# A hybrid decoder step on one core: key/value projection and compressed pages as three products of rounded parts

## The reference

```python
def key_side(h):
    kv = (rms_norm(h, kv_norm) @ w_kv).reshape(B, T, 3, 2, N_KV, HEAD_DIM)
    return kv[:, :, 0], kv[:, :, 1], kv[:, :, 2]        # raw rows, stored as outputs too

def seg_proj(seg):                                       # segments of 16 cached rows
    first = jnp.einsum('bsjcgd,cjde->bscge', seg, cmp_w[:, :CMP_STRIDE])
    second = jnp.einsum('bsjcgd,cjde->bscge', seg, cmp_w[:, CMP_STRIDE:])
    return first, second

def compress_blocks(first, second, L):                   # blocks of 32 rows, 16 apart
    blk = first[:, :nc] + second[:, 1:nc + 1] + cbias[:, None, :]
    kc = rms_norm(blk[:, :, 0], k_norm[0])
    return kc, blk[:, :, 1], e_pos
```

## Time and profile before

| | us |
|---|---|
| median of 3 runs | 2643.77 |
| range of the runs | 2643.24 to 2648.64 |
| profiled execution, its own time | 2653.37 |
| its span, first to last instruction | 2651.6 |
| TensorE busy | 2437.2 (92%) |
| VectorE busy | 1385.0 (52%) |
| ScalarE busy | 904.4 (34%) |
| mean granted TensorE clock | 0.948 |

### The profile page before, as it was taken

The page is one execution under the profiler, slowest core; times in us unless marked ns, Lnnn a source line. Parts: engine busy times, 40 slices in busy tenths (PEclk is TensorE's granted clock), DMA queues, the critical chain, the costliest instruction groups (busy, mean ns, idle before and its releaser), DMA issues. The chain is left out here.

```text
span 2651.6 us, 62243 instructions
## 1 busy us (share of the span) xinstructions
PE 2437.2 (92%) x25616; PEld 1985.1 (75%) x25616; DVE 1385.0 (52%) x2833; ACT 904.4 (34%) x2023; POOL 774.1 (29%) x460
## 2 busy tenths in 40 slices
PE   5999799986899999989999898997999978999998
PEld 3777699965799999944544385565766677999998
DVE  7216665536577773022233435774777746777600
ACT  2205344315222121110101145765888822222210
POOL 0001000110267665200000023772222204677641
PEclk8999899967899999999999987997999988999999
DMA  2121000012122223151898310005777612222231
GB/s 106 55 64 57 8 4 12 28 39 90 59 72 79 87 74 119 49 221 47 323 326 280 118 58 1 2 1 185 253 251 251 224 64 67 79 87 79 94 99 61
DMA packets 109448, 276.58 MB, mean 104 GB/s; under 512 B 13657, under 2 KB 14554, under 8 KB 107290
## 3 DMA queue, kind: packets, MB, share of 16 engines
q1 hardware_dynamic: 109210, 273.19, 30.5%
HBM read 264.42 MB, written 16.97 MB: 106 GB/s over the span
## 5 line engine op out<-in xcount | busy, mean ns | idle before, releaser
L319 PE MATMUL ps<-parts 128*128 128x288 f32 x6144 | 815.1, 295 | 7.4 <-POOL parts L288 7.4
L319 PEld LDWEIGHTS ps<-parts 128*128 128x128 f32 x6144 | 814.2, 188 | 8.1 <-POOL parts L288 8.1
L288 POOL TENSOR_TENSOR parts<-kept,parts 128x1024 fp32r<-128x1024 f32 (+1 forms) x120 | 320.7, 2673 | 119.5 <-ACT parts L283 112.3
L293 POOL TENSOR_TENSOR parts<-kept 128x1024 fp32r<-128x1024 f32 (+1 forms) x92 | 191.5, 2081 | 378.2 <-DMA kept<-in_wall 188.6
L1660 PE MATMUL ps<-mix,kept 128*128 128x512 f32 (+1 forms) x544 | 228.4, 579 | 0.3 <-DMA mix<-in_cmp_pool 0.3
L1660 PEld LDWEIGHTS ps<-mix,kept 128*128 128x128 f32 x544 | 101.4, 194 | 120.8 <-issue 119.7
L2292 POOL TENSOR_SCALAR mix<-mix 128x128 f32<-128x128 f32 (+3 forms) x128 | 136.7, 1087 | 71.9 <-DVE mix L2266 71.8
L288 POOL TENSOR_TENSOR query_rounded<-mix,query_rounded 128x1024 fp32r<-128x1024 f32 x8 | 16.0, 2000 | 466.8 <-ACT query_rounded L283 466.8
L2769 POOL TENSOR_TENSOR mix<-mix 128x512 f32<-128x512 f32 x64 | 67.0, 1047 | 252.7 <-ACT mix L2793 197.9
L1599 DVE TENSOR_TENSOR kept<-kept,ps 128x576 f32<-128x576 f32 x16 | 12.1, 756 | 245.9 <-PE ps L319 245.9
L702 PE MATMUL ps<-mix 128*128 128x288 f32 x512 | 126.4, 410 | 2.7 <-DVE mix L507 2.4
(11 more groups left out here) (470 smaller groups left out, 4870.0 us busy)
## 6 DMA issues: line engine op xcount, KB each, us to landing
mix<-in_cmp_pool SPq DMA_DIRECT2D x256, 256.0 KB, 4.9
mix<-in_slc_pool SPq DMA_DIRECT2D x192, 256.0 KB, 3.7
kept<-in_wall SPq DMA_DIRECT2D x88, 512.0 KB, 3.5
mix<-in_wall SPq DMA_DIRECT2D x48, 512.0 KB, 3.5
kept<-in_wdown SPq DMA_DIRECT2D x32, 704.0 KB, 4.1
kept<-in_slc_pool SPq DMA_DIRECT2D x64, 256.0 KB, 3.8
out_s_win<-in_state_win SPq DMA_DIRECT2D x1, 8064.0 KB
mix<-in_wkv SPq DMA_DIRECT2D x8, 768.0 KB, 10.3
```

What stands on the lines that cost most here:

```text
L288: return e.tensor_tensor(low.bitcast(F32R), whole, high, ALU.subtract)
L293: e.tensor_tensor(high.bitcast(F32R), whole, c.c("one").to_broadcast([P, whole.shape[1]]), ALU.mult).then_inc(*steps.step())
L319: mm = pe.matmul(out, l[:, f, :].bitcast(F32R), m[:, first + f, a:b].bitcast(F32R), start=first + f == 0 and k == 0, stop=last and f == n ...
```

## The change

The projection and the page products become three products of rounded parts (360 in place of 120, and 48 in place of 16 for a unit). The projection runs in three passes, one for a branch (window pass second, compressed pass last), over 24 weight pieces of 512 columns: ScalarE rounds each piece, GpSimd takes its low part. The normed tiles are rounded on ScalarE, their low parts are VectorE's. Each pass's result is copied out by both engines, key norms and turning follow inside the next pass, and GpSimd copies the values.

The pages are cut in 24 units of 11, 11 and 10 pages (a third of a sample) in four places. A unit has four quarters; ScalarE rounds a quarter into one of four buffers, VectorE writes the low part over the raw page, TensorE takes twelve products of 352 or 320 columns for it. All copies of sums (eight of 64x176 for a unit) are now ScalarE's. The key norm of the blocks takes logarithm, exponential and square on ScalarE and a Newton step on VectorE in place of square root and reciprocal. The layout of the page pool in memory puts the four row groups of a quarter together.

The copy of the old window rows (8 MB within device memory) is issued in the scan of layer 0 and no longer in this stage. The memory map grows from 52600 to 56789 words a partition, the scratch for dynamic DMA shrinks, and the rounded areas are named per stage.

The diff, cut to its core, by helper and engine.

Units, slots, and the helpers of the new stage:

```diff
+UNIT_PAGES = (11, 11, 10)
+NU = 3 * NB
...
+    passes = (1, 2, 0)
+    pieces = [(p, f) for p in range(3) for f in range(FT)]
...
+    own = lambda p, t: bank[(5 * p + t) % 8]
...
+    slot = lambda u: (3 + u) % 4
...
+    def load_unit(sp, u):
+        if u >= 4:
+            sp.wait_ge(*T.at(seg, f"mm{u - 4}"))
+        first, n = u // 3 * NPG + FIRST_PAGE[u % 3], count(u)
...
+    def round_piece(act, z):
+        act.wait_ge(piece_got[z % 4].sem, 16 * (z // 4 + 1))
+        if z >= 3:
+            act.wait_ge(*T.at(seg, f"piece{z - 3}"))
+        rounded(act, wraw[z % 4], wpart[z % 3][0]).then_inc(*A.step(f"piece{z}"))
+    def round_quarter(act, u, q):
+        n = count(u)
+        if q == 0:
+            act.wait_ge(*filled(u))
+        if u >= 1:
+            act.wait_ge(*T.at(seg, f"quarter{u - 1}_{q}"))
+        rounded(act, raw[slot(u)][:, 0:n, q], quarter[q][:, 0:n]).then_inc(*A.step(f"high{u}_{q}"))
+    def rest_quarter(v, u, q):
+        n = count(u)
+        v.wait_ge(*A.at(seg, f"high{u}_{q}"))
+        rest(v, raw[slot(u)][:, 0:n, q], quarter[q][:, 0:n], rest_of[slot(u)][:, 0:n, q]).then_inc(
+            *V.step(f"low{u}_{q}"))
```

The page products and the copies of their sums:

```diff
     def products(pe, u):
+        n, o = count(u), out_of(u)
+        if u >= 4:
+            pe.wait_ge(*A.at(seg, f"part{u - 2}"))
+        if u == 3:
+            pe.wait_ge(*A.at(seg, "part-1"))
+        for q in range(4):
+            k = q // 2
+            pe.wait_ge(*V.at(seg, f"low{u}_{q}"))
+            for j in range(4):
+                cols = slice(32 * j, 32 * (j + 1))
+                wj = [t[:, (8 * k + 4 * (q % 2) + j) * P:(8 * k + 4 * (q % 2) + j + 1) * P] for t in w_parts]
+                xj = [quarter[q][:, 0:n, cols], rest_of[slot(u)][:, 0:n, q, cols]]
+                for i, (l, r) in enumerate(((0, 0), (0, 1), (1, 0))):
+                    mm = pe.matmul(o[:, 512 * k:512 * k + 32 * n].rearrange("p (n x) -> p n x", x=32),
+                                   wj[l].bitcast(F32R), xj[r].bitcast(F32R),
+                                   start=q % 2 == 0 and j == 0 and i == 0, stop=q % 2 == 1 and j == 3 and i == 2)
+            mm.then_inc(*T.step(f"quarter{u}_{q}"))
+            if q == 3:
+                T.labels[f"mm{u}"] = T.n
...
+    def parts(act, u):
+        act.wait_ge(*T.at(seg, f"mm{u}"))
+        for second in range(2):
+            dst = (sums if u >= 0 else sums_prompt)[second]
+            for par, k in ((0, 0), (0, 1), (1, 0), (1, 1)):
+                if u < 0:
+                    src = out_of(u)[rows[second], 512 * k:512 * k + 4 * n0].rearrange(
+                        "p (a o n) -> p a o n", o=2, n=n0)[:, :, par]
+                    to = dst[rows[par], 2 * k:2 * k + 2, 0:n0]
+                else:
+                    lo, n = 8 * FIRST_PAGE[u % 3], count(u)
+                    src = out_of(u)[rows[second], 512 * k:512 * k + 32 * n].rearrange(
+                        "p (n a o s) -> p o a n s", a=2, o=2, s=8)[:, par]
+                    to = dst[rows[par], 2 * k:2 * k + 2, lo:lo + 8 * n].rearrange("p a (n s) -> p a n s", s=8)
+                act.activation(to, src, ACT.Copy).then_inc(*A.step(f"part{u}"))
...
-    def root(act, b, nb):
-        act.wait_ge(*V.at("cmp", f"mean{b}"))
-        act.activation(rr[:, 0:2 * nb], rr[:, 0:2 * nb], ACT.Sqrt).then_inc(*A.step(f"root{b}"))
...
+    def root(act, b):
+        nb = size(b)
+        act.wait_ge(*T.at(seg, f"norm{b}"))
+        act.activation(rr[:, 0:2 * nb], c.ps[0][:, 0:2 * nb], ACT.Ln, bias=c.c("eps"), scale=1.0 / HD).then_inc(*A.step())
+        act.wait_ge(*A.own())
+        act.activation(rr[:, 0:2 * nb], rr[:, 0:2 * nb], ACT.Exp, scale=-0.5).then_inc(*A.step())
+        act.wait_ge(*A.own())
+        act.activation(square[:, 0:2 * nb], rr[:, 0:2 * nb], ACT.Square).then_inc(*A.step(f"root{b}"))
```

SP's order from the 24 weight pieces on:

```diff
+            for z, (p, f) in enumerate(pieces):
+                if z >= 4:
+                    sp.wait_ge(*G.at(seg, f"piece{z - 4}"))
+                lo = f * 1536 + passes[p] * 512
+                sp.dma_start(wraw[z % 4], d["wkv"][:, lo:lo + 512]).then_inc(piece_got[z % 4].sem, 16)
+                if z == 7:
+                    sp.dma_start(w, d["wcmp"]).then_inc(*got.more())
+                    sp.dma_start(pe_, d["pe"]).then_inc(*got.more())
+                    load_unit(sp, 0)
+                if z == 13:
+                    store_pass(sp, 0)
+                if z == 21:
+                    store_pass(sp, 1)
+            sp.wait_ge(*T.at(seg, "piece23"))
+            load_unit(sp, 1)
+            store_pass(sp, 2)
+            sp.wait_ge(*T.at(seg, "segments"))
+            sp.wait_ge(*stored[2].all())
+            sp.wait_ge(*stored[1].all())
+            sp.wait_ge(*G.at(seg, "values1"))
+            sp.wait_ge(*V.at(seg, "normed1_1"))
+            sp.wait_ge(*T.at(seg, "turned1"))
+            load_unit(sp, 2)
+            sp.wait_ge(*T.at(seg, "bias"))
+            for u in range(3, NU):
+                load_unit(sp, u)
```

GpSimd's program:

```diff
+            for z in range(len(pieces)):
+                g.wait_ge(*A.at(seg, f"piece{z}"))
+                rest(g, wraw[z % 4], *wpart[z % 3]).then_inc(*G.step(f"piece{z}"))
+                if z in (10, 18):
+                    p = z // 8 - 1
+                    g.wait_ge(*A.at(seg, f"copied{p}"))
+                    g.wait_ge(*V.at(seg, f"copied{p}"))
+                    g.tensor_copy(vt[:, :, p], kv[p][:, 0:4, 256:]).then_inc(*G.step(f"values{p}"))
+                if z == 20:
+                    g.wait_ge(*A.at(seg, "weights"))
+                    rest(g, w.rearrange("p a b c -> p (a b c)"), *w_parts).then_inc(*G.step("weights"))
```

TensorE's projection, and the order of the page products behind it:

```diff
+            for z, (p, f) in enumerate(pieces):
+                pe.wait_ge(*G.at(seg, f"piece{z}"))
+                if p == 0:
+                    pe.wait_ge(*V.at(seg, f"low{f}"))
+                if p >= 1 and f == 0:
+                    pe.wait_ge(*V.at(seg, "error") if p == 1 else V.at(seg, "kept0"))
+                for t, m in tiles:
+                    if p >= 1 and f == 0 and t == 3:
+                        for steps in (V, A):
+                            pe.wait_ge(*steps.at(seg, f"copied{p - 1}"))
+                    xs = [high[:, f, t * P:t * P + m], low_part[f][:, t * P:t * P + m]]
+                    for k, (l, r) in enumerate(((0, 0), (1, 0), (0, 1))):
+                        mm = pe.matmul(own(p, t)[0:m, :], xs[l].bitcast(F32R), wpart[z % 3][r].bitcast(F32R),
+                                       start=f == 0 and k == 0, stop=f == FT - 1 and k == 2)
+                mm.then_inc(*T.step(f"piece{z}"))
+                if p >= 1 and f == 4:
+                    turn_keys(pe, p - 1)
+            pe.wait_ge(*G.at(seg, "weights"))
+            pe.wait_ge(*V.at(seg, "kept1"))
+            products(pe, 0)
+            for steps in (V, A):
+                pe.wait_ge(*steps.at(seg, "copied2"))
...
+            products(pe, 1)
...
+            prompt_products(pe)
...
+            for u in range(2, NU):
                 products(pe, u)
+                if u == 2:
+                    pe.wait_ge(*V.at(seg, "bias"))
+                    blocks_tensor(pe, -1)
+                if u % 3 == 0:
+                    blocks_tensor(pe, u // 3 - 1)
+            blocks_tensor(pe, NB - 1)
```

VectorE's order in the pages (norms and copies of the projection left out):

```diff
+            for q in range(4):
+                rest_quarter(v, 0, q)
+            evict(v, V, v.tensor_copy, 2, 1)
+            for u in (1, 2):
+                for q in range(4):
+                    rest_quarter(v, u, q)
...
+            for u in range(2, NU):
+                for q in range(4):
+                    if u + 1 < NU:
+                        rest_quarter(v, u + 1, q)
+                    if q == 0 and u % 3 == 0:
+                        blocks_vector(v, u // 3 - 1)
+                if u == 2:
+                    norms_vector(v, -1)
+                if u % 3 == 0:
+                    norms_vector(v, u // 3 - 1)
+            blocks_vector(v, NB - 1)
+            norms_vector(v, NB - 1)
```

ScalarE's order from the end of the projection on:

```diff
+            for q in range(4):
+                round_quarter(act, 0, q)
+            evict(act, A, copy, 2, 0)
+            round_quarter(act, 1, 0)
+            act.wait_ge(*T.at(seg, "segments"))
             for k in range(2):
                 for par in range(2):
                     for odd in range(2):
                         act.activation(xp[HD * odd:HD * odd + HD, k].rearrange("p (a o) j s -> p o a j s", o=2)[:, par],
+                                       c.ps[2 + k][HD * par:HD * par + HD].rearrange(
                                            "p (a s j o) -> p o a j s", a=2, j=8, o=2)[:, odd],
                                        ACT.Copy).then_inc(*A.step("segments"))
+            for q in range(1, 4):
+                round_quarter(act, 1, q)
+            parts(act, 0)
+            round_quarter(act, 2, 0)
+            parts(act, 1)
+            for q in range(1, 4):
+                round_quarter(act, 2, q)
+            parts(act, -1)
+            for u in range(2, NU):
+                if u + 1 < NU:
```

(13 more changed lines are left out.)

483 lines of the change are left out of this document (245 added, 238 removed).

## The result

The changed kernel takes 2708.69 us, the median of 4 runs (2704.73 to 2709.63), beside 2646.20 for the kernel before in the same session. The ratio is 1.0233, with a 95% interval of 1.0215 to 1.0252: slower by 62 us. The profiled execution took 2709.63 us, its span is 2707.4, against 2651.6 before, and the mean granted clock 0.934 against 0.948.

The account below looks back on a forecast made before the run. TensorE bound before; last page product at 1246.2 + 64 + 217.7 + 22.7 = 1550.6 us against 1509.8, 41 more, less 1 for the tail. Median 2643.8 + 40 = 2684 us, range 2640 to 2725.

Parts of the forecast that it names:

- from there to unit 3's copies: Start of the pages, after the projection: loads, roundings, prompt and bias products, and three idle gaps costing clock; 64 us.
- The projection: Rounded products replace whole ones, 83.2 us of them; the projection ends at 1246.2 us, 15 us won.
- the pass boundaries: Projection: at two boundaries TensorE waits for three ScalarE copies behind its own work; 1 us together.
- The ring: Steady page loop: copies, rounding, low part and three quarters of products in series; 11.05 us a unit, 217.7 for twenty.
- The signs it named: Page loop: TensorE idle 3 to 4 us a unit, copies waiting on TensorE, units 11 to 13.5 us apart, loads early.
- the price of a product with strided columns: Page products on TensorE: a rounded product takes 161 ns for 352 columns and 147 for 320.
- Rival (d): Page products reading strided runs of 32 miss one column a cycle; at half rate +130 us and more; chance 0.04.
- the hand-overs: Page loop: four hand-overs between engines in one unit's chain, 0.15 us.
- The clock: Page loop: idle gaps lower TensorE's clock, costing 1.7 us in two of three units; 22.7 us.
- Rival (a): Page loop: the clock doesn't fall, so clock losses go and the time is 2656 us; chance 0.17.
- The tail: After the last page product: new norm steps and longer copies change nothing within 1 us; the sum takes 1 off.
- The window move: Window copy goes from this stage to the scan; no compute waits for it in either place, so no cost.

Follow-up runs that it names:

- e4_fill: Changed kernel plus twelve products of constants in TensorE's gap of each unit from the fifth on; 2689.70 us, loop of twenty units 236.4.
- e12_fill_table: Changed kernel plus constant products in every unit's gap and the logarithm/exponential table set loaded once; 2688.46 us, loop 236.5.
- e2_order: Changed kernel with ScalarE rounding three quarters of the next unit, not one, ahead of this unit's copies; 2661.58 us.
- e1_table: Changed kernel with ScalarE loading the logarithm/exponential table set once, ahead of the first page rounding; 2704.33 us, loop 265.7.
- e10_window: Changed kernel with the 8 MB window copy issued again at the projection's start, not in the scan; 2724.01 us.
- e6_runs: Changed kernel with three quarters rounded ahead of copies and one table load, plus rounded pages sorted by 32-column piece; 2622.39 us.
- e11_pool: Changed kernel with reordered rounding, one table load, sorted pages, earlier bias and later norm products, plus first-quarter low parts on GpSimd from unit 4; 2626.92 us.

## Why the prediction was right, and where its size was off

The sign and its reason held. The forecast was +40 us, the runs show +62, inside the range. The steps, against the profiled execution:

| step | forecast | measured |
|---|---|---|
| last product of the projection | 1246.2 | 1245.8 (stage begun 1.8 later than before) |
| from there to unit 3's copies | 64 | 65.4 |
| twenty units at full clock | 217.7 | 236.4 (e4_fill, e12_fill_table) |
| clock in these | 22.7 | 20.6 (257.0 less 236.4) |
| last copies to the query stage | 10.5 | 13.1 (11.8 before, which the forecast read as 11.5) |

**The projection** went nearly as worked out. The first product came at 1158.3, the rounded products follow one another 0.23 us apart, and ScalarE, GpSimd (1.39 us a piece, the forecast had about 1) and VectorE stay beside TensorE. Its last product ends 15.6 us earlier than the old one's (1261.4), as forecast, and 17.4 counted from the stages' starts. That the end fits to 0.4 us is partly luck: the stage began 1.8 us later than the forecast took for granted, and TensorE has no break from its first product to its last, so the 1 us put down for the pass boundaries did not come.

**The ring** was the right reason. e2_order shows it without any change of work: the order of one engine's instructions costs 47 us, what it does to the clock included. The prediction saw that the three later quarters stand behind a wait for TensorE. The signs it named are all there: the idle gap of TensorE once a unit, ended by VectorE's low part, the copies waiting for TensorE, units 11.5 to 14.4 us apart, loads finished early.

**The term that was too small is the price of a product with strided columns.** The ring at full clock is 11.82 us a unit against 10.89, 18.7 us in twenty. The forecast scaled a product of 288 columns that lie together and gave 161 ns for 352; the rows show 180, and 165 for 320 where it had 147. Three quarters of 36 products are 0.67 us a unit, 13.4 of the 18.7. Rival (d) had asked this question with full or half rate as the only answers, and put it aside since the old page products read runs of 8 without loss; the answer is 12% more. The other 5.3 us are the hand-overs: 12.04 us in the turn shown are 2.14, 1.38, 1.63, 6.48 of products, and 0.41, not 0.15, for the latencies between them. (The forecast's own prices add up to 32.85 us a batch, not 32.7, which is less than 1 us in twenty units.)

**The clock** came out within 2 us, and by the right mechanism: full clock with the gap filled, 0.85 without. That the number fits so well is partly luck. The forecast had 1.7 us in two units of three and nothing where the norm products lie in the gap. Four turns of the kernel after:

```profile
1440.76:1452.23 11.47, 9.67 (x50) 9.39 (x51) 7.49 (x6) 6.97 (x12) 0.00 (x0) 0.85 0.68 229
1452.23:1466.53 14.30, 11.27 (x49) 10.87 (x48) 8.34 (x7) 7.18 (x13) 0.00 (x0) 0.76 0.59 203
1466.53:1478.57 12.04, 10.09 (x54) 8.99 (x52) 5.96 (x5) 11.70 (x17) 0.00 (x0) 1.00 0.71 240
1478.57:1492.03 13.46, 10.34 (x50) 10.37 (x51) 8.86 (x9) 7.08 (x12) 0.00 (x0) 0.75 0.58 195
```

Beside e4_fill's 11.28, 12.00, 12.10 and 11.28 us for the same turns they lose 0.2, 2.3, nothing and 2.2 us. The clock fell in eighteen turns of twenty, also in five of the seven with the norm products in the gap. In the first turn above the products at the lower level are those of the quarter that the norm held back (L1765 from 1442.56 on, 0.27 us apart), which costs the ring little. By the Trainium skill's rule (TensorE: Matmul & The Clock Gate, Why this matters for your kernels), taken to the letter in every unit, it would be 34 us; the run shows 20.6, so the gaps of this loop do not all pay in full. Rival (a) is out.

**The tail** was put at -1 us and is +1.3. The prediction listed logarithm and exponential and did not see that each brings a table load: the one at the exponential stands on the path (e1_table's tail is 1.3 us shorter, 11.8, which is the tail of before), the other hides in the wait for the norm product. The trace of before had such a load in the query stage.

**The window move** at nothing is not contradicted: the 1.8 us by which the stage began later lie within what its start differs by from one execution to another. What the prediction did not see is that the old place would no longer have been free (e10_window, 15 us).

The sum: 18.7 us more than forecast for the ring, 2.1 less for the clock, 1.4 more for the start, 2.6 for the tail, 0.4 less for the projection. That makes the query stage begin 59.7 us later than before where 40 was forecast. Behind it 4 us are won back in code that is the same in both, and the rest to 62 lies in how far each profiled execution stands from its median.

## What to carry to other kernels

When work is cut into pieces and several engines prepare them, write down each engine's order and look for the instruction that waits for the end of the last piece: all that stands behind it is a serial chain, however low the busy shares are, and moving two instructions ahead of it can be worth more than any price. Before an edit that takes a stall away, ask what fills the gap it leaves: here 18 us of table loads in ScalarE's loop cost nothing while they split a gap, and 26 us of loop, clock included, once the order was mended. Price a product by a row with its own access pattern, not only its own width.

## What the runs showed of the hardware

- A rounded product reading 352 columns in runs of 32, 128 apart, takes 180 ns, against about 160 when they lie together (e6_runs); 320 columns 165 against about 150.
- Twelve idle products more in each unit make the kernel 19 us faster, by the clock alone (e4_fill), and taking 18 us of table loads off ScalarE makes the loop 8.6 us longer, for the same reason (e1_table, e12_fill_table).
- A two-input instruction on VectorE started beside one on GpSimd ended only after it: 3.62 us in place of 0.75 (e11_pool).
- An 8 MB copy within device memory, issued ahead of a 256 KB load on the same queue, held the load back for 21.8 us (e10_window).
